# Layer 0's second feed-forward product by seven block products; token sums in the first phase; residual rows parked in DRAM

## The chip, the core and the metric

The kernel runs on one core of a Trainium2 chip. The metric is the device time of one execution in microseconds (us). The time before is 1638.36 us, the median of three runs (1636.8 to 1638.64).

## The reference

The reference is a two-layer backbone over 512 latent and 256 context tokens of width 1024, in float32. Every layer has attention, then a feed-forward part; each is framed by norms, shifts, scales and gates that come from a modulation vector:

```
mod   = split(silu(c) @ w_ada[layer] + b_ada[layer], 6)          # mod_c for the context from c_ctx
a     = rms_norm(h, g[0]) * (1 + mod[1]) + mod[0]
h     = h + mod[2] * rms_norm(mixer(a), g[1])                    # mixer: two kinds of attention and projections
a     = rms_norm(h, g[2]) * (1 + mod[4]) + mod[3]
f     = square(relu(a @ w_ff1[layer])) @ w_ff2[layer]            # (768 x 1024) @ (1024 x 4096) @ (4096 x 1024)
h     = h + mod[5] * rms_norm(f, g[3])
```

Layer 0 computes latent and context tokens (768 rows), the last layer gives only the 512 latent rows. The change is about the second matrix product of `f` in layer 0 and about where the modulation vectors are computed.

## The kernel before

Each engine has its own instruction list in an order written out by hand; semaphores tie the lists together. SyncE issues all DMAs in program order, so a wait there holds up every later load.

**Products in three passes.** Each float32 operand is split into a high part (ScalarE copies it rounded, `whi`, `ahi`, `hid_hi`) and a low part (VectorE subtracts, `wlo`, `alo`, `hid_lo`), and each product is three matmuls into one PSUM sum: high x high, low x high, high x low (`three_pass`, L1275 to L1277). So TensorE waits for VectorE's split of each new weight.

**Output projection of layer 0** (`output_projection`). Four weight units; the first two give columns 0 to 511 of all rows, the last two the other half, tile by tile (`wide_tile`). VectorE splits unit 9, makes the diagonals of the gates, splits unit 10, and splits unit 11 in four quarters. TensorE reads the first quarter after twelve matmuls of the second half.

**First feed-forward product of layer 0** (`block_product`, L1618). The product of the transposed weights with the tokens is done over 8 chunks of 512 hidden columns. Chunk 0 is done plainly, chunks 1 to 7 by seven block products of half-size blocks (a scheme of Strassen and Winograd), in the order p1, p4 (of the chunk before), p2, p6, p5, p7, p3. Weight sums are made on VectorE (`up_sum_of`), the split parts sit in a ring of four slots, running sums are copied out by ScalarE (`snapshot`: "a", "u1", "p5") and added on VectorE (`add_block`: c11, c22, c12); `finish` applies relu and square. The blocks lie in `hs`, and SyncE stores them to DRAM (`store`). Product p7 waits for the copy "u1", which waits for the addition of c11. VectorE also does four modulation steps a chunk.

**Modulation steps** (`modulation_step`, L3425). Rows of `w_ada` are multiplied with the silu row and summed, one instruction on 128 x 1024 elements a step. 80 steps are needed after the early part. Before, 28 are in the first product and 52 in the second; their weights come 1 MB at a time into `mod_raw` (`modulation_unit`).

**Second feed-forward product of layer 0** (`down`, `take`). Per chunk, the hidden block comes back from DRAM (`hidden`, 1.5 MB), is split (`hidden_hi`, `hidden_lo`), and is multiplied with two weight halves of 512 columns: six row tiles x 4 k x three passes per half. A PSUM bank holds one tile and half of one chunk; VectorE adds it to the running sum `xn` (`take`, L3492). The last chunk goes tile by tile (`last_down`), with the gate rows (`gate_rows`, L1270) in between, so that the boundary (`ff_boundary`) can gate, add the residual `h` and make the next norm for the first tiles while TensorE still multiplies.

**Layer 1's input projection** (`input_projection`). Nine weight units of 256 columns. Per unit u VectorE splits unit u + 2, copies turned groups, and after units 1, 2 and 4 normalises and rotates heads (`process_odd`); TensorE turns those stages after units 3, 4 and 6 (`in_groups`, L1124) and then goes on to the next unit.

Of the kernel before, what the change touches and what calls it, by code (L numbers as in the profile page):

```python
# [23 lines left out]
P = 128  # L24
D = 1024
# [62 lines left out]
def build(nc, x, ctx, cols, rows, consts, tables, na_bias, w_ada, w_ada_t, w_ff1, w_ff2, w_in_even,  # L88
# [24 lines left out]
    loads += [("ff", None)] * 2 + [("block", None)] * 14 + [("ff", None)] * 16  # L113
# [6 lines left out]
    with ExitStack() as stack:  # L120
# [84 lines left out]
        nvc = place("nvc", [P, 2, 512], F32, G)  # L205
# [22 lines left out]
        down_hi0 = place("down_hi0", [P, KT, UW], F32R, A)  # L228
        down_lo0 = place("down_lo0", [P, KT, UW], F32R, A + 8 * KB)
        mod_raw = [place("mod_raw0", [P, 2, D], F32, B + 8 * KB)]  # L230
        mod_raw += [place(f"mod_raw{i + 1}", [P, 2, D], F32, A + (16 + 8 * i) * KB) for i in range(3)]
        hid_hi = [place("hid_hi0", [P, 4, TOK], F32R, C + 12 * KB), place("hid_hi1", [P, 4, TOK], F32R, C + 36 * KB)]
        hid_lo = [place("hid_lo0", [P, 4, TOK], F32R, C + 24 * KB), place("hid_lo1", [P, 4, TOK], F32R, C)]
        hid_in = [place("hid_in0", [P, 4, TOK], F32, C + 24 * KB), place("hid_in1", [P, 4, TOK], F32, C)]
        hidden_rows = nc.dram_tensor("hidden_rows", (FF_CHUNKS, P, 4, TOK), F32, kind="Internal").ap()
# [96 lines left out]
        s_uhi = sem("hidden_hi_done")  # L332
# [22 lines left out]
        s_ulo = sem("hidden_lo_done")  # L355
# [36 lines left out]
        s_stored = [sem(f"hidden_block_stored{b}") for b in range(4)]  # L392
        s_hid = [sem("hidden_chunk_loaded0"), sem("hidden_chunk_loaded1")]
        s_mraw = [sem(f"modulation_unit_loaded{i}") for i in range(4)]
# [104 lines left out]
        W_IN1 = W_FF0 + 18  # L499
# [28 lines left out]
        def pre_squares_after(post, t, j):  # L528

            return {("post00", 2, 1): (0, 1), ("post00", 3, 1): (2, 3),  # L530
                    ("post01", 2, 1): (0,), ("post01", 3, 1): (1, 2, 3),
                    ("post10", 1, 1): (0, 1)}.get((post, t, j), ())
# [5 lines left out]
        for post, nt in (("post00", NT), ("post01", NT), ("post10", NTL), ("post11", NTL)):  # L538
            pre = next_norm[post]
            if post[5] == "0":  # L540
# [10 lines left out]
        for i, name in enumerate(sq_list):  # L551
# [4 lines left out]
        QUARTERED = {W_OUT0: 0, W_OUT0 + 3: 1, W_FF0: 2, W_FF0 + 1: 3, W_FF0 + 2: 4,  # L556
                     W_IN1: 5, W_IN1 + 1: 6, W_OUT1: 7, W_OUT1 + 3: 8, W_FF1: 9}
# [16 lines left out]
        F1_LAST, F2_LAST = 4, 16 * NT  # L574
# [72 lines left out]
        def stored_of(name):  # L647

            return s_stored[2 * int(name[1]) + int(name[2]) - 3]

# [8 lines left out]
        def mod_slot(j):  # L659

            return 0 if j < 7 else 1 + (j - 7) % 3

        def mod_value(j):

            return 16 * (j + 1) if j < 7 else 16 * ((j - 7) // 3 + 1)

        def pieces_before(j):

            return 4 * ADA_EARLY + sum(len(mod_pieces(u)) for u in mod_units[:j])
# [56 lines left out]
        def weight_parts(w):  # L726

            if w == W_FF0:
                return early_hi0, wlo[w % 2]
            if w == W_FF0 + 2:  # L730
                return down_hi0, down_lo0
            return (early_hi, early_lo) if w == W_FF1 else (whi[w % 2], wlo[w % 2])
# [4 lines left out]
        def group_bank(name):  # L737

            n = tg_index[name]
            if name[0] == "gate11":  # L740
                return 5 + 2 * name[2]
# [102 lines left out]
        def _(sp):  # L844
# [81 lines left out]
            def straight(r0, r1):  # L926
                for r in range(r0, r1):
# [7 lines left out]
                    if r == R_OUT0 + 2:  # L935

                        sp.wait_ge(s_s, S_TOTAL)
                        load_h(range(NT // 2))
# [3 lines left out]
                    sp.dma_start(dst, src).then_inc(s_raw[r % 2], 16)  # L942

            def ff_in_phases():
# [16 lines left out]
                def down(n):  # L961
                    if n == 0:
                        sp.wait_ge(s_part_lo, part_number("p2", 7) + 1)
                        sp.wait_ge(s_bsum, sum_count(7, "s3"))
                    elif n == 1:
                        sp.wait_ge(s_part_lo, part_number("p4", 7) + 1)
                    else:
                        sp.wait_ge(s_lo, W_FF0 + 2 + n - 2 + 1)
                    weights(loads_ff0 + 16 + n, w_ff2[0][n])

                def modulation_unit(j):
                    if j == 0:
                        sp.wait_ge(s_tg, tg_index["pre01", KT - 1, 1] + 1)
                    elif j < 7:
                        sp.wait_ge(s_ada, pieces_before(j))
                    elif j < 10:
                        sp.wait_ge(s_block, part_done("p3", 7))
                    else:
                        sp.wait_ge(s_ada, pieces_before(j - 2))
                    slot = mod_slot(j)  # L980
                    src = w_ada_t[mod_units[j] - ADA_FIRST]
                    sp.dma_start(mod_raw[slot][:, :, :].rearrange("p m n -> p (m n)"), src).then_inc(s_mraw[slot], 16)

                def store(c, name):
                    if c == 0:
                        sp.wait_ge(s_rsq, 2 * int(name[1]))
                    else:
                        sp.wait_ge(s_csq, finished_count(c, name))
                    rows_, cols_ = hidden_block(name)
                    sp.dma_start(hidden_rows[c][:, rows_, cols_], hs[:, rows_, cols_]).then_inc(stored_of(name), 16)  # L990

                def hidden(c):
                    for stored in s_stored:
                        sp.wait_ge(stored, 16 * (c + 1))
                    if c == 0:
                        sp.wait_ge(s_block, part_done("p5", 7))
                    elif c == 1:
                        sp.wait_ge(s_block, part_done("p4", 7))
                    else:
                        sp.wait_ge(s_f2, 12 * (c - 1))  # L1000
                    sp.dma_start(hid_in[c % 2][:, :, :], hidden_rows[c]).then_inc(s_hid[c % 2], 16)
# [5 lines left out]
                modulation_unit(0)  # L1007
                store(0, "c11")
                store(0, "c12")
                store(0, "c21")  # L1010
                store(0, "c22")
                for c in range(1, 8):
                    if c > 1:
                        store(c - 1, "c22")
                        store(c - 1, "c12")
                    up(c + 1, 0) if c < 7 else down(0)
                    if c > 1:
                        store(c - 1, "c21")
                    store(c, "c11")
                    if c == 7:  # L1020
                        hidden(0)
                    up(c + 1, 1) if c < 7 else down(1)
                    if c < 7:
                        modulation_unit(c)
                store(7, "c22")
                for j in (7, 8, 9):
                    modulation_unit(j)
                store(7, "c12")
                down(2)
                hidden(1)  # L1030
                store(7, "c21")
                down(3)
                j = 10
                for c in range(7):
                    if c:
                        hidden(c + 1)
                        down(2 * c + 2)
                    for half in range(2):
# [2906 lines left out]
```

## Time and profile before

| what | value |
|---|---|
| median of three runs | 1638.36 us |
| the profiled execution's own time | 1636.54 us |
| its span (first to last instruction) | 1634.8 us |
| mean granted clock of TensorE | 0.997 |
| chain that ended last, by engine | PE 85%, DVE 7%, ACT 2%, issue 2%, DMA 2% |
| first product of layer 0, block part | about 501.7 to 707.3 us |
| second product of layer 0 | 709.2 to 974.1 us |
| layer 1's input projection | 975 to about 1109 us |

PE is TensorE's matmuls, PEld its weight loads, DVE VectorE, ACT ScalarE, POOL GpSimd, SP or SPq SyncE and its DMA queue. "Busy" is the time in which an engine ran an instruction. In a timeline row the bracket at the end says how long the engine was idle before it and what ended the wait. Matmuls overlap, so their pace is read from start to start. The granted clock is the share of full speed that TensorE was given.

### The profile page before, as it was taken

What the parts mean: (1) busy time and instruction counts of PE and PEld (TensorE: products, weight loads), DVE (VectorE), ACT (ScalarE), POOL (GpSimd) and SP (SyncE); (2) the same over time, 40 slices, a digit from 0 to 9 for tenths busy, and PEclk for the clock granted to TensorE, in tenths of its full rate; (3) what the DMA queues carried; (4) which work ended last, traced back from release to release, by engine and by line L of the source; (5) the groups of instructions that cost most, each with busy time, mean ns of one, the idle gap of its engine ahead of it and who ended that gap; (6) DMA issues with size and microseconds to landing.
All of it is one profiled execution on the core that took longest, in us unless ns stands there. A gap on an engine that the chain in (4) does not pass through costs nothing.

```text
span 1634.8 us, 24774 instructions
## 1 busy us (share of the span) xinstructions
PE 1588.7 (97%) x9536; PEld 1376.4 (84%) x9536; DVE 1205.9 (74%) x1982; ACT 796.1 (49%) x1434; POOL 156.7 (10%) x171
## 2 busy tenths in 40 slices
PE   7999999999999999999999999999999899999997
PEld 4999888878779999988888877998877778888886
DVE  5889787675399776767778687825784777787778
ACT  5433466764475555542221255425675654445442
POOL 1000276332000000000000000003341000000000
PEclk9999999999999999999999999999999999999999
DMA  8533431013122445474665302203023133222221
GB/s 352 187 129 130 139 81 28 11 62 130 52 96 104 158 150 179 161 287 170 235 252 205 142 26 104 78 0 102 4 79 128 53 107 125 104 103 89 104 92 52
DMA packets 40132, 195.77 MB, mean 120 GB/s; under 512 B 4560, under 2 KB 15696, under 8 KB 20944
## 3 DMA queue, kind: packets, MB, share of 16 engines
q1 hardware_dynamic: 40016, 194.20, 33.4%
q8 instruction: 76, 1.25, 0.3%
q14 instruction: 40, 0.33, 0.1%
HBM read 168.75 MB, written 14.68 MB: 112 GB/s over the span
## 4 chain that ended last, share of the span: by engine, by line
PE 85%; DVE 7%; ACT 2%; issue 2%; DMA 2%; SPq 1%; POOL 0%; DVEq 0%; ACTq 0%
PE ps L1275 18%; PE ps L1277 18%; PE ps L1276 18%; PE ps L1618 12%; PE ps L1327 3%; PE ps L1448 2%; PE ps L1421 2%; PE ps L1341 2%; DMA first_raw<-in_w_ada 2%; PE ps L1361 1%; PE ps L1399 1%; PE ps L1356 1%; PE ps L1585 1%; PE ps L1409 1%; DVE nmax L3253 1%
## 5 line engine op out<-in xcount | busy, mean ns | idle before, releaser
L1275 PE MATMUL ps<-whi,ahi 128*128 128x256 f32 (+1 forms) x512 | 155.7, 304 | 3.5 <-DVE alo L3795 1.6
L1277 PE MATMUL ps<-whi,alo 128*128 128x256 f32 (+1 forms) x512 | 153.4, 300 | 0.0
L1276 PE MATMUL ps<-wlo,ahi 128*128 128x256 f32 (+1 forms) x512 | 153.4, 300 | 0.0
L1275 PE MATMUL ps<-whi,hid_hi 128*128 128x512 f32 x360 | 140.4, 390 | 0.0
L1276 PE MATMUL ps<-wlo,hid_hi 128*128 128x512 f32 x360 | 140.0, 389 | 0.0
L1277 PE MATMUL ps<-whi,hid_lo 128*128 128x512 f32 x360 | 140.0, 389 | 0.0
L1983 ACT ACTIVATE whi<-raw 128x2048 fp32r<-128x2048 f32 x33 | 63.2, 1914 | 155.9 <-PE ps L1277 143.4
L1277 PE MATMUL ps<-ahi,wlo 128*128 128x512 f32 (+2 forms) x368 | 138.1, 375 | 0.0
L1275 PE MATMUL ps<-ahi,whi 128*128 128x512 f32 (+1 forms) x336 | 127.6, 380 | 1.8 <-ACT stage L2261 1.4
L1276 PE MATMUL ps<-alo,whi 128*128 128x512 f32 (+1 forms) x336 | 127.2, 379 | 0.0
L2739 DVE TENSOR_TENSOR wlo<-raw,whi 128x2048 fp32r<-128x2048 f32 x33 | 75.6, 2291 | 60.1 <-ACT whi L1983 59.9
L1275 PEld LDWEIGHTS ps<-whi,ahi 128*128 128x128 f32 x512 | 97.8, 191 | 7.9 <-issue 2.9
L1277 PEld LDWEIGHTS ps<-whi,alo 128*128 128x128 f32 x512 | 97.8, 191 | 3.2
L1276 PEld LDWEIGHTS ps<-wlo,ahi 128*128 128x128 f32 x512 | 97.9, 191 | 3.0
L3425 DVE SCALAR_TENSOR_TENSOR ada_junk<-mod_raw,silu_rows 128x1024 bf16<-128x1024 f32 x80 | 97.5, 1218 | 0.1
L3253 DVE TENSOR_REDUCE nmax<-ps 128x1 f32<-128x768 f32 (+1 forms) x96 | 74.4, 775 | 29.3 <-PE ps L1327 28.5
L1276 PEld LDWEIGHTS ps<-wlo,hid_hi 128*128 128x128 f32 x360 | 67.6, 188 | 14.3 <-issue 0.2
L1277 PEld LDWEIGHTS ps<-whi,hid_lo 128*128 128x128 f32 x360 | 67.6, 188 | 14.1
L1275 PEld LDWEIGHTS ps<-whi,hid_hi 128*128 128x128 f32 x360 | 67.6, 188 | 14.0 <-issue 0.2
L1277 PEld LDWEIGHTS ps<-ahi,wlo 128*128 128x128 f32 x368 | 69.1, 188 | 11.3
L1618 PE MATMUL ps<-t_hi,whi 128*128 128x384 f32 x224 | 74.9, 335 | 1.1 <-ACT snap L2471 1.1
L3492 DVE TENSOR_TENSOR xn<-xn,ps 128x512 f32<-128x512 f32 x72 | 49.3, 685 | 35.5 <-PE ps L1277 35.5
(354 smaller groups left out, 4235.5 us busy)
## 6 DMA issues: line engine op xcount, KB each, us to landing
raw<-in_w_ff SPq DMA_DIRECT2D x64, 1024.0 KB, 5.0
mod_raw<-in_w_ada_t SPq DMA_DIRECT2D x28, 1024.0 KB, 5.3
raw<-in_w_ada_t SPq DMA_DIRECT2D x12, 1024.0 KB, 4.9
hidden_rows<-hs SPq DMA_DIRECT2D x32, 384.0 KB, 3.0
hid_in<-hidden_rows SPq DMA_DIRECT2D x8, 1536.0 KB, 6.5
raw<-in_w_in_odd SPq DMA_DIRECT2D x9, 1024.0 KB, 4.8
first_raw<-in_w_ada SPq DMA_DIRECT2D x8, 1024.0 KB, 19.9
raw<-in_w_in_even SPq DMA_DIRECT2D x8, 1024.0 KB, 4.9
```

The costliest lines, as they stand in the source:

```text
L1275: pe.matmul(dst, lhs[0], rhs[0], start=first, stop=False)
L1276: pe.matmul(dst, lhs[0], rhs[1], start=False, stop=False)
L1277: return pe.matmul(dst, lhs[1], rhs[0], start=False, stop=last)
L1327: last = pe.matmul(ps[:, c0:c0 + b - a], q, keys[:, a:b], start=(n == 0), stop=(n == len(passes[part]) - 1))
L1341: last = pe.transpose(dst, src[:, P * k:P * k + P], ident)
L1421: last = pe.transpose(bank(4 + b)[:, P * k:P * k + P], src[:, c0 + P * k:c0 + P * k + P], ident)
L1618: last = pe.matmul(dst, w_[:, k, a], x_[:, k, :], start=opens and k == 0 and i == 0, stop=k == 3 and i == 2, skip_group_check=name in ("p6 ...
L1983: act.activation(whi[w % 2][:, :, :], raw[r % 2][:, :, :], ACT.Copy).then_inc(s_hi, 1)
L2739: dve.tensor_tensor(wlo[w % 2][:, :, :], raw[r % 2][:, :, :], whi[w % 2][:, :, :].bitcast(F32), ALU.subtract).then_inc(s_lo, 1)
L3253: dve.tensor_reduce(nmax[:, s % 4:s % 4 + 1], ps[:, 1024 * (s % 2):1024 * (s % 2) + width], AX.X, ALU.max, negate=True).then_inc(s_mx, 1)
L3425: dve.scalar_tensor_tensor(out=ada_junk[:, :], in0=mod_raw[slot][:, mt, :], scalar=1.0, in1=silu_rows[:, s, :], op0=ALU.mult, op1=ALU.mult ...
L3492: dve.tensor_tensor(dst, dst, bank(g % 4), ALU.add).then_inc(s_f2f, 1)
```

## The change

The second product becomes seven block products too. Its 4096 x 1024 weights are read as 8 chunks of 512 x 1024, each of four 256 x 512 blocks b11, b12, b21, b22; the tokens of a chunk as four blocks a11, a12, a21, a22 of two k tiles x 384 tokens. Chunks go in two groups of four: for one product name, the parts of four chunks accumulate in one open PSUM sum (three banks, three row tiles), so 56 parts (`DOWN_PARTS`) of 18 matmuls follow each other.

```
+        DOWN_ORDER = ("p1", "p3", "p6", "p5", "p7", "p2", "p4")
+        DOWN_PARTS = [(name, 4 * g + q) for g in range(2) for name in DOWN_ORDER for q in range(4)]
+        TOKENS_OF = {"p1": "a11", "p2": "a12", "p3": "s4", "p4": "a22", "p5": "s1", "p6": "s2", "p7": "s3"}
...
+                def down_tile(m, t, first, last):
+                    name = DOWN_PARTS[m][0]
+                    chained = name in ("p6", "p7", "p4")
+                    hi, lo = down_slot(m)
+                    dst = bank(down_bank(m // 4) + t)
+                    a = slice(P * t, P * t + P)
+                    for k in range(2):
+                        for j, (x_, w_) in enumerate(((tok_hi, hi), (tok_hi, lo), (tok_lo, hi))):
+                            ins = pe.matmul(dst, x_[m % 4][:, k, a], w_[:, k, :], start=first and not chained and k == 0 and j == 0,
+                                            stop=last and k == 1 and j == 2, skip_group_check=chained)
```

Per part ScalarE makes the high parts of a weight block (`down_hi`) and of the tokens (`tokens_hi`, loaded 384 KB a part), once the ring slot of part m - 4 is free; VectorE makes the low parts. VectorE also makes the weight sums t1 (at p1), t3 and t2 (at p3), t4 (at p2 in the first group, p5 in the second), and adds the finished PSUM sums (`add_sum`, three tiles at once); ScalarE copies four of them (`copy_sum`).

The token sums s1 to s4 of a chunk are made in the first product's loop, one chunk late, and stored; s4 overwrites a12 and so waits for a12's store. VectorE's list in that loop, and at the start of the second product:

```
                     part_lo("p7", c)
+                    token_sum_of(c - 1, "s3")
+                    token_sum_of(c - 1, "s1")
+                    token_sum_of(c - 1, "s2")
                     modulation_step()
                     add_block(c, "c11")
                     part_lo("p3", c)
                     modulation_step()
                     if c < 7:
                         part_lo("p1", c + 1)
+                    token_sum_of(c - 1, "s4")
                     modulation_step()
                     part_lo("p4", c)
...
+                down_lo(0)
+                tokens_lo(0)
+                down_lo(1)
+                tokens_lo(1)
+                down_sum_of("t1", 0)
+                for name in ("s3", "s1", "s2"):
+                    token_sum_of(7, name)
+                down_sum_of("t1", 1)
+                for m in range(2, 56):
...
+                    down_lo(m)
+                    tokens_lo(m)
+                    if m == 2:
+                        token_sum_of(7, "s4")
```

SyncE's list around the start of the second product (weight blocks are 512 KB each; those of chunk 1, 2 and 3 wait for p5, p7 and p4 of chunk 7):

```
+                store(7, "a22")
+                weight_block(1, "b21")
+                weight_block(1, "b12")
+                weight_block(1, "b22")
+                weight_block(2, "b11")
+                token_part(2)
+                token_part(3)
+                weight_block(2, "b12")
+                weight_block(3, "b11")
+                weight_block(2, "b22")
+                weight_block(2, "b21")
+                weight_block(3, "b12")
+                weight_block(3, "b22")
+                weight_block(3, "b21")
+                for name in ("s3", "s1", "s2", "a12", "s4"):
+                    store(7, name)
+                modulation_unit(MOD_UP)
+                modulation_unit(MOD_UP + 1)
+                for m, (name, c) in enumerate(DOWN_PARTS):
+                    if m + 4 < len(DOWN_PARTS):
+                        token_part(m + 4)
```

The residual rows `h` are stored to DRAM (`h_rows`, 3 MB) before the first product's loop, since their place is used for token blocks, and come back in two loads (`rows_back`), the first one at part p1 of chunk 5.

The 80 modulation steps are spread anew: 16 in the output projection of layer 0, 28 in the first product as before, 12 in the second, and 24 in layer 1's input projection, where each step's rows come as a 512 KB load into one of two places, the load for step k waiting for step k - 2:

```
                 split_lo(w0 + 1)
                 gate_diagonals(f"gate{layer}0", layer, 0)
+                if layer == 0:
+                    link(dve.memset(mods[:, 2 * ADA_BOTH:96, :], 0.0))
+                    for _ in range(8):
+                        modulation_step()
                 split_lo(w0 + 2)
+                if layer == 0:
+                    for _ in range(8):
+                        modulation_step()
                 for j in range(4):
                     split_lo_quarter(w0 + 3, j)
...
                     if layer == 1 and u + 2 < n_units:
                         split_lo(w0 + u + 2)
+                    if layer == 1 and u >= 2:
+                        for _ in range(4 if u < 5 else 3):
+                            modulation_step()
...
+            def modulation_half(k):
+
+                if k < 2:
+                    sp.wait_ge(s_res, RES["01"] + NT)
+                else:
+                    sp.wait_ge(s_ada, pieces_before(MOD_DOWN) + k - 1)
+                src = w_ada_t[mod_units[MOD_DOWN + k // 2] - ADA_FIRST][:, D * (k % 2):D * (k % 2) + D]
+                sp.dma_start(mod_raw[5 + k % 2][:, :], src).then_inc(s_mraw[k % 2], 16)
```

In `last_down` the last group of four parts goes tile by tile (rows 3, 4, 5 of columns 0 to 511), and the boundary is written out: root and gating of rows 0 to 2, then 3, then the next norm, then rows 4 and 5.

## Rows read from the trace of the kernel before

**Rows 1.** The page, part 1: busy us, share of the span, instructions.
```profile
PE 1588.7 (97%) x9536; PEld 1376.4 (84%) x9536; DVE 1205.9 (74%) x1982; ACT 796.1 (49%) x1434; POOL 156.7 (10%) x171
```

**Rows 2.** Busy time by stage: window, length, PE, PEld, DVE, ACT, POOL, PEclk, DMA, GB/s.
```profile
589.00:618.00 29.00, 29.00 (x169) 29.00 (x168) 20.61 (x22) 15.97 (x18) 0.00 (x0) 1.00 0.47 161
...
775.00:807.00 32.00, 32.00 (x142) 26.50 (x142) 24.60 (x32) 6.56 (x4) 0.00 (x0) 1.00 0.54 204
...
1010.00:1070.00 60.00, 58.97 (x372) 55.85 (x371) 51.88 (x105) 26.40 (x48) 0.00 (x0) 1.00 0.19 69
```

**Rows 3.** TensorE, second product: first pass (ns min/median/max, first and last start), then timeline.
```profile
L1275 PE MATMUL ps<-whi,hid_hi x360: 389/389/793, 725.6 to 973.2; 128*128 128x512 f32 x180
...
709.15 0.47 PE L1275 MATMUL ps<-down_hi,hid_hi 128*128 128x512 f32 x1 [1.83 <-issue]
...
948.69 3.59 PE L1270 MATMUL ps<-diag,kons 128*128 128x512 f32 x8
```

**Rows 4.** Timeline (start us, us, engine): two modulation steps; then the output projection.
```profile
164.63 1.23 DVE L3186 SCALAR_TENSOR_TENSOR ada_junk<-raw,silu_rows 128x1024 bf16<-128x1024 f32 x1
...
165.90 1.23 DVE L3186 SCALAR_TENSOR_TENSOR ada_junk<-raw,silu_rows 128x1024 bf16<-128x1024 f32 x1
...
419.71 2.29 DVE L2739 TENSOR_TENSOR wlo<-raw,whi 128x2048 fp32r<-128x2048 f32 x1 [17.10 <-ACT whi L1983]
...
424.29 1.90 DVE L2750 TENSOR_TENSOR wlo<-raw,whi 128x512 fp32r<-128x512 f32 x3 [2.29 <-ACT whi L1993]
...
429.11 0.39 PE L1275 MATMUL ps<-whi,mla_hi 128*128 128x512 f32 x1
```

**Rows 5.** Timeline, first product: chunk 4 (VectorE, ScalarE, SyncE), SyncE a chunk earlier, TensorE in chunk 1.
```profile
581.44 0.35 SPq L947 DMA_DIRECT2D raw<-in_w_ff  x1
...
599.32 1.22 DVE L3425 SCALAR_TENSOR_TENSOR ada_junk<-mod_raw,silu_rows 128x1024 bf16<-128x1024 f32 x1
...
600.47 0.95 DVE L3466 TENSOR_TENSOR hs<-snap,ps 128x768 f32<-128x768 f32 x1
...
603.36 0.81 ACT L2471 ACTIVATE snap<-ps 128x768 f32<-128x768 f32 x1 [0.18 <-PE ps L1618]
...
610.56 0.35 SPq L947 DMA_DIRECT2D raw<-in_w_ff  x1
...
616.76 1.22 DVE L3445 TENSOR_TENSOR up_sum<-raw 128x1024 f32<-128x1024 f32 x1
...
519.82 0.44 PE L1618 MATMUL ps<-t_hi,whi 128*128 128x384 f32 x1 [1.15 <-ACT snap L2471]
```

**Rows 6.** DMA issues (count, KB each, median us to landing) at 715.5, 703.2, 487.5 and 1042.9 us.
```profile
hidden_rows<-hs SPq DMA_DIRECT2D x1, 384.0 KB, 11.9
...
mod_raw<-in_w_ada_t SPq DMA_DIRECT2D x3, 1024.0 KB, 8.2
...
hidden_rows<-hs SPq DMA_DIRECT2D x2, 384.0 KB, 2.8
...
raw<-in_w_in_odd SPq DMA_DIRECT2D x1, 1024.0 KB, 4.7
```

**Rows 7.** Timeline, boundary to layer 1: root of the norm (VectorE), first turning (TensorE).
```profile
971.35 0.17 DVE L2794 TENSOR_SCALAR chv<-ss 128x4 f32<-128x4 f32 x1
...
975.09 0.66 PE L1141 MATMUL ps<-kons,xn 128*128 128x128 f32 x4 [1.03 <-ACT xn L2034]
```

**Rows 8.** Timeline, layer 1's input projection: TensorE's turnings and wait; splits on VectorE.
```profile
1028.67 0.39 PE L1275 MATMUL ps<-whi,ahi 128*128 128x256 f32 x1 [1.03 <-DVE wlo L2739]
...
1040.53 2.29 DVE L2739 TENSOR_TENSOR wlo<-raw,whi 128x2048 fp32r<-128x2048 f32 x1
...
1046.05 0.93 PE L1124 MATMUL ps<-kons,stage 128*128 128x128 f32 x7
...
1068.12 2.29 DVE L2739 TENSOR_TENSOR wlo<-raw,whi 128x2048 fp32r<-128x2048 f32 x1
...
1080.22 1.25 PE L1124 MATMUL ps<-kons,stage 128*128 128x128 f32 x10
```

More of the change, by code:

```diff
@@ new lines, in down_number, with down_block, down_source, down_slot @@
+        def down_number(name, c):
+            return DOWN_PARTS.index((name, c))
+        def down_block(q, name):
+            k = 2 * int(name[1]) - 2
+            return down_land[q][int(name[2]) - 1][:, k:k + 2, :]
+        def down_source(name, c):
+            return down_block(c % 4, "b11" if name == "p4" and c >= 4 else HELD_IN[name])
+        def down_slot(m):
+            i = (UP_PARTS + m) % 4
+            return [x[i // 2][:, 4 * (i % 2):4 * (i % 2) + 4, :].rearrange("p k n -> p (k n)").rearrange("p (k n) -> p k n", n=512)
+                    for x in (whi, wlo)]
@@ L671, in up_raw, with token_source @@
+        def token_source(name):
+            if name in ("s2", "s3"):
+                return (s2_block if name == "s2" else s3_block)[:, :, :]
+            return hidden_of({"s1": "a21", "s4": "a12"}.get(name, name))
         def up_raw(c, half):
@@ L739, in group_bank @@
             n = tg_index[name]
+            if name[0] == "gate01":
+                return 3 + 4 * (n % 2)
             if name[0] == "gate11":
@@ L1025, in ff_in_phases @@
[L1025 to L1038, printed above, removed]
-                        if c and half:
-                            down(2 * c + 3)
-                        taken = 4 * ADA_EARLY + 28 + 8 * c + 4 * half + 4
-                        while j < len(mod_units) and pieces_before(j - 2) <= taken:
-                            modulation_unit(j)
-                            j += 1
+                sp.wait_ge(s_xn, XN["pre01"] + NT)
@@ new lines, in ff_in_phases, with input_loads @@
+                rows_back(1)
+            def input_loads():
+                k = 0
+                for u in range(2, len(ODD_KINDS)):
+                    straight(loads_in1 + u, loads_in1 + u + 1)
+                    if u < 5:
+                        continue
+                    for _ in range(2 if u == 5 else 5):
+                        modulation_half(k)
+                        k += 1
+                while k < 2 * (len(mod_units) - MOD_DOWN):
+                    modulation_half(k)
+                    k += 1
@@ L1260, in wide_tile, with gate_rows @@
                 last.then_inc(s_g, 1)
-            def gate_rows(tag, layer):
-                for s in streams[layer]:
+            def gate_rows(tag, layer, which=None):
+                for s in which or streams[layer]:
                     for half in range(2):
@@ L3476, in halves_lo, with token_sum_of @@
                                       ALU.subtract).then_inc(s_cross_lo, 1)
[L3478 to L3487 removed]
+                def token_sum_of(c, name):
+                    first, second, done = {"s3": ("a11", "a21", "c12"), "s1": ("a21", "a22", "c22"),
+                                           "s2": ("s1", "a11", "c11"), "s4": ("a12", "s2", "c21")}[name]
@@ new lines, in ff_in_phases @@
+                post, pre = "post01", "pre10"
+                settled = lambda: dve.wait_ge(s_gated, gated[0])
+                back = lambda i: dve.wait_ge(s_hback[i], 16)
+                columns = lambda t: gate_columns_of(post, t, 0, 512, 0)
+                post_root(post, 0, 3)
+                columns(0)
+                settled()
+                back(0)
+                residual(post, 0)
+                add_sum(13, "c21", "q43", 0)
+                columns(1)
+                settled()
@@ new lines, in ff_in_phases @@
+                residual(post, 1)
+                columns(2)
+                post_root(post, 3, 1)
+                settled()
+                residual(post, 2)
+                columns(3)
+                settled()
+                residual(post, 3)
+                add_sum(13, "c21", "q44", 1)
+                pre_root(pre, 0, 4)
+                normalize(pre, 1, 2)
+                normalize(pre, 1, 3)
+                split_lo_quarter(W_IN1, 0)
+                add_sum(13, "c21", "q45", 2)
@@ L3582, in ff_by_blocks @@
+                post_root(post, 4, 2)
+                settled()
+                back(1)
+                residual(post, 4)
+                residual(post, 5)
+                pre_root(pre, 4)
             def ff_by_blocks():
```

702 lines of the change are left out of this document (423 added, 279 removed).

## The prediction

> **What bounds the kernel now.** I read the busy shares first, then stages, then single waits. TensorE is busy for 97% of the span and VectorE for 74% [rows 1]; in the three stages that the change touches most, TensorE has no gaps and VectorE is busy for 20.6 of 29 us (first product of layer 0's feed-forward), 24.6 of 32 us (second product) and 51.9 of 60 us (part of layer 1's input projection) [rows 2]. So matmuls taken away count in full, while VectorE work that is added or moved counts where it, or what it waits for, becomes later than TensorE needs it. The last stage has next to no room.
>
> **What is removed.** The second product has 8 chunks x 2 halves x 6 row tiles x 4 k x 3 passes = 1152 matmuls of 512 columns. Seven block products of three row tiles, two k and three passes over 8 chunks are 7 x 8 x 18 = 1008: 144 fewer. The first of the three passes has 360 matmuls from 725.6 to 973.2 us; less some 3.0 us of the gate product at 948.69, that is 244.6/(3 x 359) = 0.227 us each [rows 3]. 144 x 0.227 = **-32.7 us**. The form of the matmul stays, so does the gate product; the granted clock is 1.00 in all three stretches [rows 2] (the 2.4 GHz level), and I take it as unchanged.
>
> **Output projection (VectorE takes 16 modulation steps here).** A step that follows another costs 1.27 us from start to start (164.63 to 165.90) [rows 4]. The first eight lie in 17.1 us in which VectorE waited for ScalarE (before 419.71) [rows 4]: 10.2 us, free; their two 1 MB loads wait for the last transposed probabilities and still land in time. The second eight stand between two weight splits: from 419.71 + 2.21 = 421.9 us, 7 x 1.27 + 1.15 = 10.0, then 0.7 for the first quarter (512 of the 2048 columns that take 2.29): 432.6, where TensorE wanted it at 429.11 [rows 4]. **+3.5 us** (3 to 4). ScalarE's quarters and the gate copies queue behind with room; VectorE's later pauses absorb the rest.
>
> **First product.** Four token sums per chunk are added, 128x768 like the block addition (0.95 us) [rows 5], 1.04 when each waits for the last. Three of them (2.9 us) stand between the p7 split and the c11 addition. ScalarE's copy "u1" waits for that addition, and p7 for the copy. In chunk 1 TensorE already waited 1.15 us for it (519.82) [rows 5], so +2.6 us. In a later chunk the copy starts at 603.36, having waited 0.18 us for TensorE, takes 0.81, and p7 starts a product (29.12/7 = 4.2 us) after that moment, at 607.4: moving the copy by 2.9 uses up the slack. Behind it runs a loop: copy u1 (start S) -> p1 split (S+1.8) -> fourth token sum -> modulation step -> p4 split, done at S+6.2 -> SyncE issues the next weight half -> landing 5.3 us later (610.56 to 615.9, before the sum at 616.76) -> s1 and s2 sums, p6, p5, p7 splits (S+23.2: from 616.76 - 29.12 = 587.64 to the end of the p7 split at 599.32 it is 11.7 us) -> three token sums, step, addition, ScalarE's relu and square (together 6.7) -> the copy again: 29.9 us, against the 29.12 us at which chunks follow each other (581.44 to 610.56) [rows 5]. 0.8 us x 6 chunks = 4.8. Together **+7.4 us**; low bound 2.6 (weights 0.8 us earlier), high 12 (1.6 per chunk).
> SyncE's own queue: each load of a weight half now also stands behind the store of s4; that is in the loop.
>
> **Between the products.** TensorE waited 1.83 us here (709.15) [rows 3]; the first new part's splits end near 706, so that goes. But at the third part (m = 2) VectorE waits for the store of a12 of chunk 7, so that s4 may overwrite it. SyncE issues that store behind all sixteen 512 KB weight blocks, fourteen of them after 694.8 us and six only after 707.3, and behind three stores. From 701.8 to 713.5 us it issues 8.1 MB. In the nearest row 384 KB stored behind loads of 2.6 MB landed after 11.9 us, with an empty queue after 2.8 [rows 6]. Three 1 MB loads issued from 703.2 on had a median of 8.2 us, so some 0.34 to 0.42 MB per us [rows 6]: the store lands at 722 to 726, I take 723. VectorE stands from 716 to 723, then s4, t1, and the two splits of m = 3 (4.1 us) end at 727.1; TensorE wanted them at 719.7. Behind s4's store SyncE then puts 2 MB of modulation rows before the tokens of m = 4: those land near 732.8, +3.3. The p3 parts take VectorE 2.0 + 2 sums of 1.14 = 4.3 us against 18 x 0.227 = 4.1: +1.2 over the group. Total 12.0, less the 1.83: **+10 us**; bounds +1 (the store lands at once) and +14.
> After that VectorE needs 12.6 to 19 us per group of four parts where TensorE needs 16.3, over a ring of four slots: no stall expected.
>
> **Boundary to layer 1.** Only the last group's tiles are ordered row by row. From the start T of the last group: splits of the last part done T+4.0 (needed T+4.1), then a root, four gatings, four residual additions, a second root and two additions from PSUM, at the durations that they have before 971.35, bring the root of the next norm to T+15.9; the first turning by TensorE follows 3.7 us after a root's start (971.35 to 975.09), so at T+19.5. The group's 72 matmuls end at T+16.3: 3.2 us idle, against 1.03 us now [rows 7]. **+2.1 us** (0 to 6). The residual rows return from DRAM some 90 us earlier, so their load costs nothing.
>
> **Layer 1's input projection (24 modulation steps, a 512 KB load each, two slots).** The load for step k+2 is issued when step k is done. With 1024 KB landing in 4.7 us and 384 KB in 2.8 [rows 6], 512 KB lands in about 3.2 (estimate between them). Four steps then take 1.2 + 3.3 + 1.2 + 1.3 = 7.0 us, not 5.0, and 8.8 or 9.5 where a 1 MB weight load stands ahead. The split of unit 4 was already awaited by TensorE (1.03 us at 1028.67) [rows 8]; four steps follow it, then the normalisation that ended at 1040.5. TensorE turns its result at 1046.05 [rows 8]: with 7.0 to 8.8 it ends at 1047.5 to 1049.3, and unit 5's split (2.3 us) at 1049.9 to 1051.6 where 1046.9 was wanted: +3 to +5. Units 6 and 4's keys: 7.0 + 7.0 to 9.5 of steps come before the normalisation that ended at 1068.1 and was turned at 1080.22 [rows 8]; TensorE is at 1083.3 to 1085.2, VectorE at 1086.3 to 1090.5; with unit 7's split +4 to +6.5. Three steps before unit 8's split: +2.5. Sum 9.7 to 13.9, I take **+12 us**. Low bound 1.6: if loads were never awaited, four steps cost 5.0 and only 0.9 + 0.3 + 0.4 remain. The steps end near 1120 us, before the odd attention needs VectorE.
>
> **Sum.** -32.7 + 3.5 + 7.4 + 10 + 2.1 + 12 = **+2.3 us** on the profiled execution's own 1636.54 us (span 1634.8 and 1.7 around it). The median of the runs is 1.8 us above that execution; on it, 1638.4 + 2.3 = 1640.7, forecast **1641**. 0.2% is 3.3 us, about what a measurement of this kernel can tell from no change: this forecast is "no change", with the gain handed back in five places.
>
> **Rivals.**
> *A, the transfers hide.* If the store of a12 lands early and the loads of steps are not awaited, the terms become 3.5 + 2.6 to 7.4 + 1 + 2.1 + 1.6 to 8: 11 to 22, time 1617 to 1628. For it: the queues are idle for 80% of layer 1's stretch [rows 2]; against it, a ring of two with a wait per step cannot prefetch, and the 11.9 us row. With the store alone early it is -7: 1632.
> On that one the Trainium skill, "DMA: Bandwidth & Descriptors", section "Queues, rings and completion order", says that completion is not in the order of issue and later descriptors may finish before earlier ones; it would allow that 1632. The 11.9 us row speaks against it for a store behind full-width loads.
> *B, slower: the two-slot ring.* Layer 1's input projection is VectorE-bound for its first 90 us. If a half-unit load lands in 4.7 us as a whole unit does, each burst grows by 1.5 us, and four bursts stand before unit 8's split; the term is 18 instead of 12, and the first product's loop, by the same lateness of loads (0.8 more per chunk), 12 instead of 7.4. That is 1651. It decides from about 3.9 us of landing on. For it: 88% VectorE share before the steps arrive [rows 2].
> *C, the seven products don't run at TensorE's rate:* VectorE has 2.0 us of splits, up to two sums and an addition per 4.1 us part. If they were paced at 4.3 over all 56 parts, +12 more: 1653. Against it: only the p3 groups reach 4.3.
>
> **Chances.** Forecast 0.48, own range 1634 to 1648 (faster 0.12, same 0.18, slower 0.18); A 0.29 (all faster); B 0.18 and C 0.05 (slower). Together faster 0.41, same 0.18, slower 0.41. All low bounds together give 1614, all high ones 1656; the range with 8 in 10 is 1619 to 1652.
>
> **What would show it.** The 1008 matmuls at 0.227 us; TensorE idle before the first wlo quarter of the second half of the output projection (3.5 us); p7 waiting for the u1 copy, 0.8 us in each chunk; one wait of 7 us or more of VectorE for the a12 store near its third part, and TensorE idle near 720 to 735; TensorE waiting for wlo and for the normalised stage of units 1 and 4 in layer 1, with VectorE idle before steps until the load of their rows. The forecast is wrong if the a12 store lands within 4 us, if VectorE never idles before a modulation step in layer 1, or if TensorE's matmul count times 0.227 us isn't the whole gain.

## The result, and the profile after

The kernel with the change takes 1658.4 us (median of four runs, 1655.8 to 1659.7) against 1637.6 us (four runs of the kernel before, 1636.4 to 1638.6): ratio 1.0124, 95% interval 1.0111 to 1.0137, slower. The forecast was 1641. The profiled execution took 1659.68 us against 1636.54: +23.1, where the working came to +2.3.

The page, part 1 (against [rows 1]), then part 2's row of the granted clock:

```profile
PE 1576.1 (95%) x9392; PEld 1362.2 (82%) x9392; DVE 1283.9 (77%) x2047; ACT 846.7 (51%) x1515; POOL 156.8 (9%) x171
...
PEclk9999999999999999999999999989999999999999
```

The instruction count is lower by exactly the 144 matmuls. TensorE's idle time is the span less its busy time: 1657.9 - 1576.1 = 81.8 us, before 46.1. That is +35.7, and the waits in the prediction added to +35.0. But its busy time fell by 12.6 us, not by 32.7. So the waits as a sum came out as forecast, and 20 us went somewhere else: the matmuls that remain were slower. The 8 in the clock row is the trail.

Windows around pauses (window, length, PE, PEld, DVE, ACT, POOL, PEclk, DMA, GB/s), the last one against the third of [rows 2]:

```profile
432.00:436.00 4.00, 2.51 (x6) 2.03 (x7) 4.00 (x8) 0.00 (x0) 0.00 (x0) 0.57 0.00 0
436.00:439.00 3.00, 3.00 (x8) 2.32 (x8) 1.13 (x2) 0.00 (x0) 0.00 (x0) 0.50 0.93 292
439.00:442.00 3.00, 3.00 (x13) 2.42 (x13) 1.29 (x2) 2.77 (x6) 0.00 (x0) 0.94 0.14 57
...
530.00:534.00 4.00, 3.94 (x12) 3.94 (x13) 3.02 (x3) 2.60 (x4) 0.00 (x0) 0.50 0.27 98
...
745.00:750.00 5.00, 4.07 (x10) 3.23 (x11) 3.05 (x3) 0.00 (x0) 0.00 (x0) 0.50 1.01 366
...
1006.00:1009.00 3.00, 3.00 (x9) 2.31 (x8) 0.55 (x1) 2.42 (x3) 0.00 (x0) 0.50 0.83 328
...
1055.00:1060.00 5.00, 4.75 (x15) 4.76 (x16) 2.57 (x5) 1.02 (x2) 0.00 (x0) 0.50 0.46 149
...
1097.00:1102.00 5.00, 5.00 (x19) 4.53 (x20) 4.59 (x5) 1.74 (x4) 0.00 (x0) 0.55 0.12 25
```

```profile
1010.00:1070.00 60.00, 54.88 (x331) 50.86 (x330) 45.23 (x88) 23.72 (x45) 0.00 (x0) 0.94 0.40 141
```

Behind these pauses of TensorE the granted clock stands at half (the 1.2 GHz level) for some us in which TensorE is fully busy and does half the matmuls: 8 in the 3 us from 436, 13 in the 3 us from 439. It happened in eight places; the stretches at half lasted 3.4, 6.8 or, around the longest pause, 10.2 us. With busy time x (1 - granted clock) summed over half-microsecond windows of the span, 17.3 us are lost so, and 1.6 in the kernel before (all of it before 15 us). The difference, 15.7 us, is most of the 20.1.

The pauses themselves, from TensorE's timeline (before: 1.15, 1.83, 1.03 us in [rows 5, 3, 7]):

```profile
433.49 0.79 PE L1460 MATMUL ps<-whi,mla_hi 128*128 128x512 f32 x1 [3.89 <-DVE wlo L2966]
...
745.93 0.77 PE L1827 MATMUL ps<-whi,tok_hi 128*128 128x512 f32 x1 [11.28 <-DVE tok_lo L3690]
...
975.77 0.47 PE L1326 MATMUL ps<-kons,xn 128*128 128x128 f32 x1 [3.15 <-ACT xn L2226]
...
1096.95 1.33 PE L1309 MATMUL ps<-kons,stage 128*128 128x128 f32 x5 [5.69 <-DVE token L3288]
```

The others of this kind are 4.10 us before p7 of chunk 1, 2.61 before part 4, 2.52 before unit 2 of layer 1, 4.01 before its first turning and 2.38 before unit 8. Behind the 2.61 us alone the clock stayed at 1.00. The stages, measured from one landmark of TensorE's list to the next (landmarks before: 485.16, 709.15, 975.09, 1108.77; after: 492.41, 720.88, 975.77, 1131.94):

| stage | forecast | measured | of it longer pauses | half clock by the windows |
|---|---|---|---|---|
| up to chunk 0 of the first product | +3.5 | +7.3 | 3.9 | 2.9 |
| first product | +5.6 | +4.5 | 3.0 - 1.8 | 2.4 |
| second product and boundary | -18.8 | -11.1 | 17.4 | 2.0 |
| layer 1's input projection | +12 | +22.5 | 13.3 | 9.9 |
| from layer 1's attention to the end | 0 | 0.0 | | |

(Forecast of the second row: +7.4, less the old wait of 1.83 us at its end; of the third: -32.7 + 11.8 + 2.1.)

### The profile page after: what moved, and what is told of

It reads as the page before. It is cut to its first block, busy times and chain, and to the rows that moved or that the text cites. A ratio compares the mean times of both kernels' runs of the same rounds, so it can differ in the third digit from the quotient of the medians.

```text
span 1657.9 us, 24945 instructions
## 1 busy us (share of the span) xinstructions
PE 1576.1 (95%) x9392; PEld 1362.2 (82%) x9392; DVE 1283.9 (77%) x2047; ACT 846.7 (51%) x1515; POOL 156.8 (9%) x171
## 4 chain that ended last, share of the span: by engine, by line
PE 47%; DVE 13%; ACT 5%; DMA 5%; issue 4%; SPq 0%; DVEq 0%; ACTq 0%
PE ps L1827 12%; PE ps L1460 8%; PE ps L1462 8%; PE ps L1461 8%; PE ps L1633 2%; PE ps L1803 2%; PE ps L1606 2%; DMA raw<-in_w_ff 2%; DMA mod_raw<-in_w_ada_t 1%; ACT whi L2632 1%; PE ps L1584 1%; DVE ada_junk L3370 1%; DVE wlo L3620 1%; PE ps L1594 1%; DVE hs L3680 1%
## 5 line engine op out<-in xcount | busy, mean ns | idle before, releaser
L1462 PE MATMUL ps<-whi,alo 128*128 128x256 f32 (+1 forms) x496 | 147.8, 298 | 0.0
L1827 PE MATMUL ps<-whi,tok_hi 128*128 128x512 f32 x336 | 133.0, 396 | 15.6 <-DVE tok_lo L3690 15.3
L1827 PE MATMUL ps<-whi,tok_lo 128*128 128x512 f32 x336 | 131.5, 391 | 0.0
L1827 PE MATMUL ps<-wlo,tok_hi 128*128 128x512 f32 x336 | 131.5, 391 | 0.0
L3370 DVE SCALAR_TENSOR_TENSOR ada_junk<-mod_raw,silu_rows 128x1024 bf16<-128x1024 f32 x80 | 97.6, 1220 | 29.2 <-DMA mod_raw<-in_w_ada_t 27.2
L2666 ACT ACTIVATE whi<-down_land 128x1024 fp32r<-128x1024 f32 x56 | 59.3, 1058 | 107.9 <-PE ps L1827 101.2
L3686 DVE TENSOR_TENSOR wlo<-down_land,whi 128x1024 fp32r<-128x1024 f32 x56 | 68.4, 1221 | 28.9 <-ACT whi L2666 28.4
L1827 PEld LDWEIGHTS ps<-whi,tok_hi 128*128 128x128 f32 x336 | 63.6, 189 | 32.2 <-DVE wlo L3686 13.1
L1462 PEld LDWEIGHTS ps<-ahi,wlo 128*128 128x128 f32 x368 | 70.3, 191 | 11.5
L1460 PEld LDWEIGHTS ps<-ahi,whi 128*128 128x128 f32 x336 | 64.2, 191 | 15.5 <-DVE wlo L2955 4.4
L1803 PE MATMUL ps<-t_lo,whi 128*128 128x384 f32 x224 | 75.8, 338 | 0.0
L1803 PE MATMUL ps<-t_hi,wlo 128*128 128x384 f32 x224 | 75.7, 338 | 0.0
```

What stands on the lines that cost most here:

```text
L1460: pe.matmul(dst, lhs[0], rhs[0], start=first, stop=False)
L1462: return pe.matmul(dst, lhs[1], rhs[0], start=False, stop=last)
L1803: last = pe.matmul(dst, w_[:, k, a], x_[:, k, :], start=opens and k == 0 and i == 0, stop=k == 3 and i == 2, skip_group_check=name in ("p6 ...
L1827: ins = pe.matmul(dst, x_[m % 4][:, k, a], w_[:, k, :], start=first and not chained and k == 0 and j == 0, stop=last and k == 1 and j == 2 ...
L2666: act.activation(down_slot(m)[0], down_source(name, c), ACT.Copy).then_inc(s_dhi, 1)
L3370: dve.scalar_tensor_tensor(out=ada_junk[:, :], in0=weights, scalar=1.0, in1=silu_rows[:, s, :], op0=ALU.mult, op1=ALU.mult, accum_out=mods ...
```

## The experiments

All medians, with the ratio to the kernel before on the same chip. That kernel gave 1637.4, 1637.9 and 1638.7 us in the three sets of runs, so a difference between kernels of different sets is uncertain by about 1 us.

**Pauses filled.** The direct test of the clock: matmuls into an unused PSUM bank where TensorE waits.

```
+ def filler(n, dst, lhs, rhs):
+     for _ in range(n):
+         pe.matmul(dst, lhs, rhs, start=True, stop=True, skip_group_check=True)
+ if m in (3, 4): ... filler({3: 44, 4: 8}[m], bank(3), down_slot(m)[0][:, 0, 0:P], down_slot(m)[0][:, 0, :])
```

> The changed kernel with matmuls into an unused PSUM bank (results never read) where TensorE waited: 14 before the first quarter split of the output projection's second half, 18 before p7 of chunk 1, 44 and 8 before parts 3 and 4 of the second product, 14 at the boundary, 14 and 22 before the turnings of layer 1. Nothing that others wait for is earlier. Theory (the granted clock falls to half after a TensorE pause of some us and the work behind it runs at half speed, 15.7 us over eight places): the six filled places keep their clock, 12 to 13 us come back, median about 1645, ratio to before about 1.004. Rival (the slower pace has to do with transfers or with the waits themselves): no change, 1658, or some us more where a filler delays the matmul behind it.

Measured 1653.5 (ratio 1.0093, 1.0076 to 1.0110): 4.9 us less than the changed kernel. Windows over three filled places:

```profile
432.00:439.00 7.00, 6.27 (x28) 4.85 (x27) 6.82 (x11) 2.02 (x5) 0.00 (x0) 1.00 0.31 109
526.00:535.00 9.00, 8.00 (x47) 7.68 (x46) 7.84 (x12) 5.33 (x7) 0.00 (x0) 1.00 0.33 108
1050.00:1060.00 10.00, 8.77 (x53) 8.53 (x54) 5.82 (x7) 2.87 (x5) 0.00 (x0) 1.00 0.55 201
```

The mechanism holds: at four of the six filled places the clock stays at 1.00, and adding 134 matmuls made the kernel faster. At the other two a pause was left behind the fillers (2.83 us before part 4, 2.77 before the second turning), and the clock fell to half for 3.4 us again. The size doesn't hold: the windows say that 9.3 us of loss went (12.7 in the first four stages of the table, less 3.3 that came new at the start and near 1310 us), and 4.9 came back. Where is seen at the landmarks. Output projection: 2.3 us come back of 2.9. First product: 228.5 us in both, though the 2.4 us of loss are gone; TensorE does chunk 1 sooner and then waits again for the copy "u1", 0.8 us in chunk 2. Second product: nothing, the tokens of part 4 land at their own time. Layer 1: 4.0 of 7.0. So a lost clock costs only as far as TensorE is the bound behind it, as chunk 1 shows.

**The pause by itself,** in the kernel before. GpSimd, idle there, holds TensorE before three chunks of the second product; in the second kernel TensorE runs fillers meanwhile.

```
+ pool.wait_ge(s_f2, 12 * c)                     # c in (2, 4, 6)
+ pool.memset(hs[:, 0:n, :], 0.0).then_inc(s_gap, 1)      # n = 4, then 2
  def down(c):
+     pe.wait_ge(s_gap, 2 * GAPS.index(c) + 2)   # second kernel: 17 filler matmuls ahead of it
```

> The kernel before, with TensorE held for about 4.3 us by GpSimd at three places of the second product (before chunks 2, 4 and 6), nothing else changed. Theory: each pause costs its length and some 3 us more, for the matmuls behind it run at half the granted clock for about 6.8 us: 3 x 7.4 = +22, median 1660. Rival (a pause costs its length): 3 x 4.3 = +13, median 1651.

> The same three holds, but TensorE runs 17 matmuls into an unused PSUM bank (3.9 us) during each. Theory: only the length is left, +13, median 1651, granted clock 1.00 through the second product. Rival: as the kernel with the holds alone, within 1 us.

Measured 1656.9 (1.0117, 1.0102 to 1.0132) and 1651.7 (1.0087, 1.0072 to 1.0102). TensorE behind the first hold, empty, then filled:

```profile
779.57 0.47 PE L1277 MATMUL ps<-whi,hid_hi 128*128 128x512 f32 x1 [4.46 <-DVE wlo L2755]
```

```profile
780.00:783.50 3.50, 3.50 (x11) 2.68 (x10) 0.00 (x0) 1.71 (x2) 0.00 (x0) 0.54 0.87 364
783.50:787.00 3.50, 3.50 (x17) 2.89 (x16) 1.91 (x4) 1.15 (x1) 0.00 (x0) 0.98 0.02 9
```

```profile
781.00:784.50 3.50, 3.50 (x16) 2.85 (x16) 0.70 (x2) 1.74 (x2) 0.00 (x0) 1.00 0.90 379
```

(The releaser in the first row is the profile's guess; VectorE had been done, and the hold ended last.) The same three pauses (4.46, 4.37 and 4.37 us) cost 19.5 us empty and 14.3 filled: 1.7 us each for the clock where TensorE is the bound. That is about half of the 3 us expected: the half clock lasted 3.4 us behind two of the holds, and 6.8 around the third, of which 2.4 fell into the pause itself. With fillers the clock stayed at 1.00 at all three holds, but not through the whole second product: it was at half from 709.86 for 3.4 us, behind a pause of 1.83 us (709.29) that the kernel before has too (709.15), there with the clock at 1.00.

**The output projection.**

```
  split_lo(w0 + 2)
- for _ in range(8):  modulation_step()
+ for _ in range(4):  modulation_step()      # 3 more behind the first product(t), 1 behind pre_root(pre, 0)
```

> The changed kernel; of the second eight modulation steps in layer 0's output projection, four stay between the two weight splits, three go behind the addition of the first tile's half, where VectorE waited 4.4 us, one goes behind the third. Theory: the pause of 3.9 us and the 2.9 us lost at half clock behind it both go, median 1652. Rivals: a pause costs its length alone, 1654.5; or the moved steps push the residual additions and turn up before the first product, 1658.

Measured 1651.0 (1.0080, 1.0066 to 1.0093): 7.4 us for a pause of 3.9. Its landmark is 485.25 (before 485.16): the whole +7.3 of this stage hung on four steps in the wrong place.

**Chunk 1.**

```
  halves_lo("t3")
- halves_lo("t4")                # and one modulation_step(): both now behind add_block(1, "c11")
```

> The changed kernel; in chunk 1 of the first product VectorE makes the low parts of t4 and one modulation step after the addition of c11 and not before it (3.1 us of work out of the chain to the copy u1). Theory: TensorE's pause before p7 falls from 4.1 to about 1.1 us and the half clock behind it goes (2.4 us): median 1653. Rival (the loop of the later chunks takes up what chunk 1 gives): 1658.

Measured 1655.6 (1.0108, 1.0094 to 1.0122), 2.8 us back. TensorE's waits in the first product, in total, number of times, longest:

```profile
PE ps L1803 <- ACT snap L2645: 3.4, 3, 1.6
```

The pause before p7 fell to 1.5 us and a new one of 1.55 came up in chunk 2: half of the gain, and the rival's half. The 2.8 us are not sure, for the interval of this ratio overlaps that of the changed kernel (1.0111 to 1.0137); the first product itself took 226.2 us instead of 228.5.

**The second product's start.** First s4 of chunk 7 in its own place, then SyncE's list in another order as well.

```
+ dst = snap[1][:, :, :] if (name, c) == ("s4", 7) else token_source(name)
...
- blocks b11 b12 b22 b21 of chunks 1 to 3; store(7, ...) x5; modulation_unit x2; token_part(4), (5), ...
+ what p1 and p3 need, with token_part(2) to (5) in between; at m == 3 store(7, ...) x5; then b21 x3, modulation_unit x2
```

> The changed kernel, with s4 of chunk 7 written to a place of its own (the copy place of p5), so that VectorE doesn't wait for the store of a12. Theory (the wait of 11.5 us for this store is what delays parts 3 and 4): the pause before part 3 goes; parts 4 and on still stand behind the stores and 2 MB of modulation rows in SyncE's list, so TensorE's 15 us of pauses here fall to about 5: median 1648. Rival (the queues are full anyway, and the tokens of part 4 land at 752 whatever VectorE does): 1656 to 1658.

> The changed kernel with s4 of chunk 7 in its own place (as the run with that alone, 1652.6) and SyncE's list in another order: the tokens of parts 4 and 5 and the blocks that p1 and p3 need come first, the stores of chunk 7 behind part 3, the blocks b21 and 2 MB of modulation rows behind those. Theory (the order in the queue made the tokens of part 4 late, 11.1 us): the pause before part 4 and its half clock go: 12 to 13 us below 1652.6, median 1640. Rival (the bytes are the bound: 8 MB at 0.41 MB per us until 740 in any order): 6 us, 1646.

Measured 1652.6 (1.0091, 1.0076 to 1.0106) and 1641.6 (1.0023, 1.0013 to 1.0033). TensorE's waits from 700 to 960 us, first kernel, then second:

```profile
PE ps L1828 <- DVE tok_lo L3694: 12.4, 3, 11.1
```

```profile
PE ps L1830 <- DVE tok_lo L3696: 1.3, 2, 0.9
```

With the overwrite gone, a pause as long as the first came one part later: the tokens of part 4 stood in SyncE's list behind the stores and 2 MB of modulation rows. So the wait for the store had hidden a second one. The list is worth 11 us, the place 5.8, in this sequence. The rival's bound, all bytes by 740 us in any order, would have given 1646; it did not hold, for what p1 and p3 don't need could go later.

**Layer 1's input projection.** Five places for the rows, in two orders of SyncE's list, and the steps left out.

```
+ mod_raw places 5 to 9 at C + 24 KB, C + 28 KB, B, B + 4 KB, B + 8 KB
+ ring = [k % 5 if k < 12 else k % 2 for k in range(24)]
  for u in range(2, 9): straight(loads_in1 + u, loads_in1 + u + 1)
+     # loads of steps behind unit u: first order {4: 2, 5: 5, 6: 5, 7: 4, 8: 4}, second {4: 2, 5: 3, 6: 4, 7: 3}
```

> The changed kernel; the 24 steps of layer 1's input projection stay where they are, but their rows go through five places instead of two (two from step 13 on), and their loads are issued as soon as a place is free. Theory (the two-place ring is what makes bursts of four steps last 9 us and not 5): VectorE's waits of up to 5 us before steps go, TensorE's pauses before the turnings (4.0 and 5.7 us) fall to about 1 us or less: 12 to 14 us back, median 1645. Rival (the 24 steps themselves, 30 us of VectorE, set the time here): 3 to 5 us back, median 1654.

> The changed kernel with five places for the rows of the 24 steps in layer 1's input projection (two from step 13 on), and SyncE's list so ordered that no weight unit stands behind a load that waits for a late step (the run before it had that fault: TensorE waited 10 us for unit 8). Theory (waits for the rows made the stage late): pauses before both turnings and before the last split go, with the half clock behind them: 11 to 13 us, median 1646. Rival (the steps' own 30 us of VectorE are the cause): 4 to 6 us, 1653.

> The changed kernel without the 24 steps of layer 1's input projection and without their 12 MB of loads (the columns of the modulation vector that they give stay zero). It prices that part. Theory: the stage takes again what it took before the change and 3 us at half clock: 19 us back, median 1639. Rival (something else in the stage is slower, the residual rows or the boundary): 10 us back or less, 1648.

Measured 1653.8 (1.0099, 1.0084 to 1.0115), 1645.4 (1.0045, 1.0032 to 1.0059) and 1639.6 (1.0007, 0.9998 to 1.0016). The first was my own fault: the load of unit 8 stood behind loads that wait for late steps, and TensorE waited for its split:

```profile
1100.14 0.80 PE L1469 MATMUL ps<-whi,ahi 128*128 128x512 f32 x1 [10.03 <-DVE wlo L2964]
```

In the right order the same five places are worth 13.0 us. VectorE's waits for rows, in the changed kernel and in this one:

```profile
DVE ada_junk L3370 <- DMA mod_raw<-in_w_ada_t: 27.2, 13, 5.0
```

```profile
DVE ada_junk L3380 <- DMA mod_raw<-in_w_ada_t: 13.6, 8, 3.2
```

All 24 steps together, with their loads, cost 18.8 us (the run without them, which gives no modulation columns). So 13 of these went with the two-place ring, places and order of the loads together. The other 6 are left with five places; they are not the steps' own time alone, for TensorE still waits 3.26 us for the last split (1095.29).

**All mends,** and the same with fillers in the two pauses left.

> All mends in one kernel: steps apart in the output projection, chunk 1's chain, s4 of chunk 7 in its own place, SyncE's order in the second product, five places and order in layer 1's input projection (4, 4, 4, 2, 2, 4, 4 steps). Theory (each cause is separate): 7.4 + 2.8 + 16.8 + 12 below 1658.4, median 1619 to 1621, ratio to before 0.989. Rival (one stall gone lets the next appear): 1628 or more.

> The kernel with all mends, and matmuls into an unused PSUM bank in the two pauses that are left in it, 14 at the boundary to layer 1 (3.2 us of pause) and 10 before unit 2 of the input projection (2.5 us). Theory (each of the two is followed by 3.4 us at half clock, which costs 1.4 to 1.7): 3 us below the kernel without them. Rival (TensorE waits for VectorE again a little later in that stage, so that the clock costs nothing there): within 1 us of it.

Measured 1616.0 (0.9865, 0.9852 to 0.9879) and 1613.5 (0.9849, 0.9836 to 0.9863). Singly the mends gave 7.4 + 2.8 + 16.8 + 13.0 = 40.0, together 42.4 (each against the kernel before of its own set: 41.9 and 43.6): the causes are separate to within 2 us. The kernel with all mends also has the steps of layer 1 spread otherwise (2, 2, 4, 4 behind the last four units, not 3 each), which no run tries by itself. TensorE's waits from 400 to 1100 us in the first of them, the longest five:

```profile
PE ps L1336 <- ACT xn L2236: 4.1, 2, 3.4
PE ps L1813 <- ACT snap L2655: 3.9, 4, 1.7
PE ps L1470 <- ACT stage L2446: 2.5, 1, 2.5
PE ps L1470 <- DVE wlo L2967: 2.2, 3, 1.0
PE ps L1470 <- DVE alo L3075: 1.4, 3, 0.6
```

The 24 fillers give 2.5 us more; the ranges don't touch (1615.96 to 1617.06, 1613.34 to 1614.01). But not both pauses were worth filling. At the boundary the clock was at half from 948.79 for 6.8 us without fillers (3.0 us lost) and stayed at 1.00 with them. Before unit 2 it was the other way round, first without, then with fillers:

```profile
978.00:984.00 6.00, 3.47 (x16) 2.82 (x16) 2.20 (x2) 5.77 (x7) 0.00 (x0) 1.00 0.44 157
```

```profile
978.00:981.50 3.50, 3.50 (x10) 2.74 (x9) 0.65 (x1) 2.82 (x4) 0.00 (x0) 0.51 0.94 328
```

The empty pause of 2.53 us had left the clock at 1.00. The ten fillers began only behind a wait of 1.93 us, and they and what followed ran at half. So the expectation that each of the two is followed by half clock held for one. By the landmarks 1.7 of the 2.5 us were gained in layer 1's input projection, behind the boundary (138.5 to 136.8 us), and 0.7 in the first product, where nothing was changed.

So the seven products are worth having: second product and boundary take 237.7 us with all mends, where they took 265.9 before, and the kernel is 22.7 us under the kernel before (1638.7 in these runs), 25.2 with fillers, once little waits for them.

## Why the prediction was wrong

**The step that failed** is in "What is removed": "the granted clock is 1.00 in all three stretches [rows 2] ..., and I take it as unchanged". Five terms then added pauses, 2 to 12 us a term, to a TensorE that so far had none above 1.83 us in these stages, and each was priced at its length. The runs show the price that was missing: with the holds it was 1.7 us on top of the length; in the changed kernel 1.4 to 2.9 us at eight of nine places by the windows, 17.3 us in sum, 15.7 more than before. The Trainium skill, "TensorE: Matmul & The Clock Gate", section "HAM oscillation — how this bites in real kernels", describes it: a wait between bursts of matmuls lets the clock fall back, and the next burst starts at half rate. The trace agrees at eight of the nine longer pauses, with the numbers above; I had weighed only a rule on transfers.

Term by term:
- *Matmuls removed, -32.7.* Count right, pace right: from part 9 to part 45 (776.52 to 923.40) a part of 18 matmuls takes 4.08 us, 0.2267 each against 0.2271 of [rows 3]. Only the first parts of p3 take 4.40 us, as the "+1.2 over the group" of the term between the products had it. Seven products keep TensorE's rate (rival C is out).
- *Output projection, +3.5.* The pause was 3.89 us. The cost was 7.4.
- *First product, +7.4.* The chunk 1 pause came (4.10, from 1.15), the loop not: from chunk to chunk 29.12, 29.13, 29.56, 29.30 and 29.34 us, in sum 0.9 over 29.12, where I had 4.8. The chain of 29.9 us took a landing of 5.3 us for the weight halves; they landed after 4.8 (median of this stage, before 5.3), which leaves 29.4.
- *Between the products, +10.* The place was right, the size not. The prediction lets the second product start at 707.3, and it started at 720.88; so its times have to be read 13.6 us later here. The store's landing, taken as 723, becomes 736.6; it was 741.6. With the 11.9 us of [rows 6] the issue would have been at 724.7; it was at 729.1, for SyncE first had to take the stores of s3, s1 and s2 (the last of them made at 726.9) and stood 2.1 us at the issue of the last. It landed after 12.5 us. So the row's 11.9 us was near, and the issue 4.4 us late. VectorE waited 11.5 us, not 7. The tokens of part 4, forecast at 732.8, here 746.4, came at about 752.7. The rule on completion order that the prediction weighed (the Trainium skill, "DMA: Bandwidth & Descriptors", section "Queues, rings and completion order") allows a store to finish before loads issued ahead of it; here it did not. The store of s2, issued at 726.91, took 13.7 us, and that of a12, issued at 729.10, landed 1 us behind it.

```profile
741.69 0.96 DVE L3680 TENSOR_TENSOR hs<-hs,s_block 128x768 f32<-128x768 f32 x1 [11.53 <-DMA token_rows<-hs]
```

- *Boundary, +2.1.* The pause was 3.15 us where 3.2 was forecast; the half clock behind it was not.
- *Layer 1's input projection, +12.* The 512 KB load landed after 4.5 us, not 3.2: over the 3.9 from which rival B was to decide. B's 18 is near what leaving the steps out gives (18.8), but by luck: the longer pauses of this stage are 13.3 us, and the rest of its +22.5 is mostly half clock (9.9). B's other half, a slower first product, was wrong. Rival A is out too: VectorE waited 11.5 us for the store and 27.2 for rows. The page, part 6:

```profile
mod_raw<-in_w_ada_t SPq DMA_DIRECT2D x24, 512.0 KB, 4.5
```

Pauses: forecast 35.0, measured 35.7. That the sum agrees is partly luck: the first product was 3.5 too high, the wait between the products 3.5 too low. All the high bounds of the terms together gave 1656, and 1658.4 lies above even that: a term was missing. Of the 20.8 us between forecast and measurement in the profiled execution, 15.7 stand in the windows as half clock and 0.7 as pauses; the other 4 or so have no row. What the clock alone costs at the changed kernel's end is less sure than that: fillers in six of eight places gave back 4.9 us.

## What to carry to other kernels

Where TensorE has run without pauses, price a new wait at its length and a half clock behind it, here 1.4 to 2.9 us where it came, with nothing as the low bound, and look at the granted clock in short windows, for the mean (0.984) hides it. When a list is issued in order, a wait taken away shows the next one in that list: mend place and order together. A ring of two can't load ahead of bursts of four steps: it cost 27.2 us of waits over 24 steps of 1.2 us. Look first for SBUF that is free at that moment.

## What was not expected of the hardware

- The length of a pause alone does not tell whether the clock falls. After 2.38 and 2.52 us (before units 8 and 2 of layer 1, changed kernel) it was at half for 3.4 us. After 2.61 us (part 4, changed kernel), 2.53 us (unit 2, all mends) and 3.20 us (boundary, five places in the right order) it stayed at 1.00. The pause of 1.83 us before the second product was followed by half clock in the kernel with filled holds and not in the kernel before. What decides it is not shown here.
- Longer pauses had 3.4 or 6.8 us at half, and the 11.3 us pause had 10.2 us, most of it while TensorE was idle.
- Matmuls whose result nobody reads can pay for themselves: 14 at the boundary kept the clock, and with ten more that did not the kernel became 2.5 us faster.
- A 384 KB store behind a full queue landed after 12.5 us; the next one, issued at 742.7 when the queue had run empty, after 3.1 us.
